# Matmuls in another order, and three sums of squares through short matmuls, in a one-core hybrid trunk

## What is computed

```python
def rms_norm(x, g):
    return x * lax.rsqrt(jnp.mean(x * x, axis=-1, keepdims=True) + NORM_EPS) * g

def sqrelu_mlp(h, w_up, w_down):            # 2048 -> 8192 -> 2048
    return jnp.square(jax.nn.relu(h @ w_up)) @ w_down

h = x
for layer in range(2):
    hn = rms_norm(h, mix_norm[layer])
    mix = attention(hn, ...) if layer == 0 else rglru_block(hn, ...)
    h = h + mix
    h = h + sqrelu_mlp(rms_norm(h, mlp_norm[layer]), w_up[layer], w_down[layer])
return rms_norm(h, final_norm)
```

## Time and profile before

| | us |
|---|---|
| median of 3 runs | 1996.98 (1996.09 to 1997.16) |
| profiled execution | 1997.17 |
| its span, first to last instruction | 1995.2 |
| PE busy | 1981.6 (99%), 11532 matmuls |
| PE weight loads busy | 1735.6 (87%), 11532 |
| DVE busy | 1368.6 (69%) |
| ACT busy | 1062.1 (53%) |
| mean granted TensorE clock | 0.999 of full speed |

### The profile page before, as it was taken

One profiled execution on the slowest core, in us unless ns is written; L12 is line 12 of the kernel. 1 busy time (PEld: TensorE's weight loads), 2 busy tenths in 40 slices (PEclk: granted clock), 3 DMA queues, 4 the chain that ended last, 5 costly groups with the idle time before them and its releaser, 6 DMA issues.

```text
span 1995.2 us, 33969 instructions
## 1 busy us (share of the span) xinstructions
PE 1981.6 (99%) x11532; PEld 1735.6 (87%) x11532; DVE 1368.6 (69%) x1575; ACT 1062.1 (53%) x1446; POOL 7.3 (0%) x11
## 2 busy tenths in 40 slices
PE   9999999999999999999999999999999999999998
PEld 8898888888888888888888888888888888888887
DVE  7998676556656665666789997766566556656664
ACT  6666554444444444445588885544444444444453
POOL 1000000000000000000000000000000000000000
PEclk9999999999999999999999999999999999999999
DMA  8544565666555656556566655555665566555652
GB/s 286 158 127 153 175 200 185 195 187 191 188 187 177 198 188 189 178 179 200 190 190 189 189 169 188 191 190 189 191 188 184 195 180 198 186 188 177 199 175 95
DMA packets 365307, 368.17 MB, mean 185 GB/s; under 512 B 11472, under 2 KB 363856, under 8 KB 365136
## 3 DMA queue, kind: packets, MB, share of 16 engines
q1 hardware_dynamic: 364976, 365.53, 58.1%
q0 software_dynamic: 288, 2.10, 0.3%
HBM read 365.48 MB, written 2.10 MB: 184 GB/s over the span
## 4 chain that ended last, share of the span: by engine, by line
PE 94%; DVE 3%; ACT 2%; issue 1%; DMA 0%; DVEq 0%; SPq 0%; ACTq 0%
PE ps L1307 61%; PE ps L1310 30%; DVE w_lo L812 1%; ACT h L467 1%; PE aux L1327 1%; PE aux L1328 1%; PE aux L1329 1%; ACT w_hi L370 0%; DVE h L923 0%; DMA h<-x_l_dram 0%; DVE h L934 0%; PE aux L1382 0%; DVE u L826 0%; DVE pt L939 0%; DVE u L899 0%
## 5 line engine op out<-in xcount | busy, mean ns | idle before, releaser
L812 DVE TENSOR_TENSOR w_lo<-w_raw,w_hi 128x1024 fp32r<-128x1024 f32 x678 | 815.7, 1222 | 337.8 <-ACT w_hi L370 336.7
L370 ACT ACTIVATE w_hi<-w_raw 128x1024 fp32r<-128x1024 f32 x678 | 701.3, 1053 | 449.9 <-PE ps L1310 446.8
L1307 PE MATMUL ps<-xn,w_hi 128*128 128x512 f32 x2880 | 907.5, 396 | 2.5 <-DVE xn L880 2.3
L1307 PE MATMUL ps<-mid,w_hi 128*128 128x512 f32 x2544 | 799.4, 396 | 1.0 <-DVE w_lo L812 0.5
L1310 PEld LDWEIGHTS ps<-xn,w_lo 128*128 128x128 f32 x2880 | 541.7, 188 | 128.2
L1310 PEld LDWEIGHTS ps<-mid,w_lo 128*128 128x128 f32 x2544 | 477.9, 188 | 113.0
L1310 PE MATMUL ps<-xn,w_lo 128*128 128x256 f32 x2880 | 566.8, 278 | 0.0
L1310 PE MATMUL ps<-mid,w_lo 128*128 128x256 f32 x2544 | 500.1, 278 | 0.0
L1307 PEld LDWEIGHTS ps<-xn,w_hi 128*128 128x128 f32 x2880 | 439.6, 189 | 3.5 <-issue 2.9
L1307 PEld LDWEIGHTS ps<-mid,w_hi 128*128 128x128 f32 x2544 | 387.2, 189 | 1.8 <-DVE w_lo L812 0.9
L826 DVE TENSOR_TENSOR u<-ps,half 128x512 f32<-128x512 f32 x169 | 116.5, 690 | 155.3 <-ACT half L383 136.0
(11 more groups left out here) (168 smaller groups left out, 757.4 us busy)
## 6 DMA issues: line engine op xcount, KB each, us to landing
w_raw<-mlp_w_up_dram SPq DMA_DIRECT2D x256, 512.0 KB, 3.8
w_raw<-mlp_w_down_dram SPq DMA_DIRECT2D x256, 512.0 KB, 3.6
w_raw<-b_w_in_dram SPq DMA_DIRECT2D x64, 512.0 KB, 4.9
w_raw<-a_w_qkv_dram SPq DMA_DIRECT2D x40, 512.0 KB, 5.5
w_raw<-a_w_o_dram SPq DMA_DIRECT2D x32, 512.0 KB, 4.6
w_raw<-b_w_out_dram SPq DMA_DIRECT2D x32, 512.0 KB, 4.8
h<-x_l_dram SPq DMA_DIRECT2D x4, 512.0 KB, 8.6
gate_raw<-b_gate_a_w_dram SPq DMA_DIRECT2D x8, 256.0 KB, 2.8
```

The costliest lines, as they stand in the source:

```text
L370: nc.scalar.activation(w_hi[:, s, :, :], w_raw[:, slot, :, :], ACT.Copy).then_inc(hi_ready, 1)
L812: nc.vector.tensor_tensor(w_lo[:, s, :, :], w_raw[:, slot, :, :], w_hi[:, s, :, :].bitcast(F32), ALU.subtract).then_inc(lo_ready, 1)
L1307: nc.tensor.matmul(ps[:, 2 * half_i + b, :], hi[:, k, b * PART:(b + 1) * PART], operand[:, :, kt, :], start=kt == 0, stop=False)
```

## The change

In products a flag in_turn gives another order: for b = 0, for all four k, long and then short, and then the same for b = 1. It is set for all chunks of both MLPs but the first pair of each, for all chunks of the recurrent quads 1 to 7, and for chunks 0 to 2 of six attention pairs. All other chunks keep the order.

stats(n) is replaced by short_stats(n) for n = 1, 2 and 3 (both MLP norms and the recurrent block's norm); stats(0) stays. For it ScalarE copies acc to the high part of xc_split and VectorE subtracts to get the low part, both behind the first split of the pair (next_hi and next_lo with s = 0), and TensorE multiplies a float32r matrix of ones, ones_r, with the two parts of the two halves, four matmuls of 256 columns. GpSimd sets ones_r in a third memset, for which TensorE's first loop waits as well.

```diff
             nc.gpsimd.memset(eps[:, :], EPS).then_inc(consts_set, 1)
+            nc.gpsimd.memset(ones_r[:, :].bitcast(F32), 1.0).then_inc(consts_set, 1)
...
+            def acc_split_hi(n):
+                act.wait_ge(acc_ready, 8 * (n + 1))
+                nc.scalar.activation(xc_split[:, 0, :, :], acc[:, :, :], ACT.Copy).then_inc(acc_hi, 1)
+
             def up_step(q, half_i, j, relus, norm=None):
-                for s in range(3):
+                next_hi(q, half_i, 0)
+                if norm is not None:
+                    acc_split_hi(norm)
+                for s in (1, 2):
                     next_hi(q, half_i, s)
...
+            def acc_split_lo(n):
+                dve.wait_ge(acc_hi, n)
+                nc.vector.tensor_tensor(xc_split[:, 1, :, :], acc[:, :, :], xc_split[:, 0, :, :].bitcast(F32),
+                                        ALU.subtract).then_inc(acc_lo, 1)
...
-            def products(q, half_i, s, operand, ready_sem, ready, late=False):
+            def products(q, half_i, s, operand, ready_sem, ready, late=False, in_turn=False):
...
-                for k in range(CH_KT):
+                def long(k, b):
                     kt = s * CH_KT + k
-                    for b in range(2):
-                        nc.tensor.matmul(ps[:, 2 * half_i + b, :], hi[:, k, b * PART:(b + 1) * PART],
-                                         operand[:, :, kt, :], start=kt == 0, stop=False)
-                    for b in range(2):
-                        last = nc.tensor.matmul(ps[:, 2 * half_i + b, TOK:2 * TOK], lo[:, k, b * PART:(b + 1) * PART],
-                                                operand[:, 0, kt, :], start=False, stop=kt == KT - 1)
+                    nc.tensor.matmul(ps[:, 2 * half_i + b, :], hi[:, k, b * PART:(b + 1) * PART],
+                                     operand[:, :, kt, :], start=kt == 0, stop=False)
+
+                def short(k, b):
+                    kt = s * CH_KT + k
+                    return nc.tensor.matmul(ps[:, 2 * half_i + b, TOK:2 * TOK], lo[:, k, b * PART:(b + 1) * PART],
+                                            operand[:, 0, kt, :], start=False, stop=kt == KT - 1)
+
+                if in_turn:
+                    for b in range(2):
+                        for k in range(CH_KT):
+                            long(k, b)
+                            last = short(k, b)
+                else:
+                    for k in range(CH_KT):
+                        long(k, 0)
+                        long(k, 1)
+                        short(k, 0)
+                        last = short(k, 1)
                 last.then_inc(wts_used, 1)
...
+            def short_stats(n):
+                pe.wait_ge(acc_lo, n)
+                for b in range(2):
+                    nc.tensor.matmul(x3[:, 0:TOK], ones_r[:, :], xc_split[:, 0, b, :], start=b == 0, stop=False)
+                    last = nc.tensor.matmul(x3[:, 0:TOK], ones_r[:, :], xc_split[:, 1, b, :], start=False, stop=b == 1)
+                last.then_inc(stats_done, 1)
...
-            pe.wait_ge(consts_set, 2)
+            pe.wait_ge(consts_set, 3)
...
-                pair(q, half_i, *qkv, between)
+                pair(q, half_i, *qkv, between, (0, 1, 2) if g_before is not None else ())
...
-                quad(base, *operand, {3: lambda: stats(norm)})
+                whole = tuple(range(CHUNKS))
+                quad(base, *operand, {3: lambda: short_stats(norm)}, (), whole)
                 with pe.Fori(1, 4) as i:
-                    quad(i + base, *operand)
+                    quad(i + base, *operand, None, whole)
...
-            quad(QB_IN, *lru_in, {3: lambda: stats(2)})
+            quad(QB_IN, *lru_in, {3: lambda: short_stats(2)})
             with pe.Fori(1, GATE_BLOCKS) as n:
-                quad(n + QB_IN, *lru_in, {0: lambda: gates(n - 1)})
+                quad(n + QB_IN, *lru_in, {0: lambda: gates(n - 1)}, tuple(range(CHUNKS)))
```

More of the change, by code:

```diff
@@ L154, in build @@
         ones = sb("ones", [PART, PART])
+        ones_r = sb("ones_r", [PART, PART], F32R)
         eps = sb("eps", [PART, 1])
@@ L224, in build @@
         consts_set = sem("consts_set")
+        acc_hi, acc_lo = sem("acc_hi"), sem("acc_lo")
         stats_done, rms_ready = sem("stats_done"), sem("rms_ready")
@@ L698, in lru_quad @@
                 next_hi(q, 0, 0)
+                if isinstance(n, int) and n == 0:
+                    acc_split_hi(2)
                 if before:
@@ L1044, in _ @@
                 residual_step(i + QB_WO, 1, i * 2 + 1, (1, "mlp0"))
+            def acc_split_lo(n):
+                dve.wait_ge(acc_hi, n)
+                nc.vector.tensor_tensor(xc_split[:, 1, :, :], acc[:, :, :], xc_split[:, 0, :, :].bitcast(F32),
+                                        ALU.subtract).then_inc(acc_lo, 1)
             def up_step(q, half_i, j, relus, norm=None):
-                for s in range(3):
+                next_lo(q, half_i, 0)
+                if norm is not None:
+                    acc_split_lo(norm)
+                for s in (1, 2):
                     next_lo(q, half_i, s)
@@ L1197, in lru_quad @@
                 next_lo(q, 0, 0)
+                if isinstance(n, int) and n == 0:
+                    acc_split_lo(2)
                 if before:
@@ L1312, in products, with pair, quad @@
                 last.then_inc(wts_used, 1)
-            def pair(q, half_i, operand, ready_sem, ready, between=None):
+            def pair(q, half_i, operand, ready_sem, ready, between=None, in_turn=()):
                 for s in range(CHUNKS):
-                    products(q, half_i, s, operand, ready_sem, ready)
+                    products(q, half_i, s, operand, ready_sem, ready, in_turn=s in in_turn)
                     if between and s in between:
                         between[s]()
-            def quad(q, operand, ready_sem, ready, between=None, between_b=None):
-                pair(q, 0, operand, ready_sem, ready, between)
-                pair(q, 1, operand, ready_sem, ready, between_b)
+            def quad(q, operand, ready_sem, ready, between=None, in_turn=(), in_turn_b=None):
+                pair(q, 0, operand, ready_sem, ready, between, in_turn)
+                pair(q, 1, operand, ready_sem, ready, None, in_turn if in_turn_b is None else in_turn_b)
@@ L1446, in mlp @@
                 operand = (xn, xn_ready, 8 * norm)
-                quad(base, *operand, {3: lambda: stats(norm)})
+                whole = tuple(range(CHUNKS))
+                quad(base, *operand, {3: lambda: short_stats(norm)}, (), whole)
                 with pe.Fori(1, 4) as i:
-                    quad(i + base, *operand)
+                    quad(i + base, *operand, None, whole)
                 with pe.Fori(0, 4) as i:
-                    quad(i + (base + 4), mid, mid_ready, mid_base)
+                    quad(i + (base + 4), mid, mid_ready, mid_base, None, whole)
                 with pe.Fori(1, GROUPS) as g:
                     with pe.Fori(0, 4) as i:
-                        quad(g * 8 + i + base, *operand)
+                        quad(g * 8 + i + base, *operand, None, whole)
                     with pe.Fori(0, 4) as i:
-                        quad(g * 8 + i + (base + 4), mid, mid_ready, g * PAIRS + mid_base)
+                        quad(g * 8 + i + (base + 4), mid, mid_ready, g * PAIRS + mid_base, None, whole)
             mlp(QB_MLP0, 1, MID_MLP0)
```

## The result

The changed kernel takes 2015.37 us (median of 4 runs, 2014.38 to 2015.57), the kernel before in the same session 1997.07: the ratio is 1.0091 with a 95% interval of 1.0079 to 1.0104. It is slower by 18 us, where the forecast was 1995.8 and the range ended at 2008.

The account below looks back on a forecast made before the run. TensorE's matmul stream was taken to bound the kernel. From the profiled 1997.17 us, order zero, sums -1.14 and start zero gave 1996.0, or 1995.8 against the median; own range 1993 to 2001, whole range 1967 to 2008.

Parts of the forecast that it names:

- What bounds the kernel: TensorE's stream: matmuls busy 99% of the span, PE never waits, 1 ns in a group of four matmuls is 2.3 us.
- One surcharge of 13 to 14 ns per matmul, wherever it stands: Every matmul costs that over its columns, whatever its neighbours, so the new order changes nothing: zero; chance 0.42.
- The range of that step: Bounds on the new order's effect: 14 ns a group down (32 us) to 10 ns a group up (23 us).
- the upper case: The new order is slower, 8 ns a group (2014) or 10 ns (2019); chance 0.19.
- Rival A: Alternating long and short saves 7 ns a group, 16 us, giving 1980; chance 0.39.
- Rival B: Eight matmuls in a row into one PSUM bank cost 8 ns a group, 18 us, giving 2014; chance 0.19.
- The sums: Short float32r sums of squares in three norms save 0.38 us each, 1.14 us in all, with their operand's preparation hidden.
- The start: An added memset delays the warm-up 0.1 to 0.2 us, hidden; the half clock could shift -1.7 to +1.7 us; taken as zero.
- The rule on the ports: Skill rule: weight loads take no bandwidth from the running matmul; estimates a group at 650 ns where the trace has 697.

Follow-up runs that it names:

- e7: Changed kernel with eight longs, then eight shorts, in every in-turn chunk of the first MLP and only the first in-turn chunk of the second; 2006.81 us.
- e5: Changed kernel plus short matmuls in the gates' form and operands behind the sums of squares, 24 in the first MLP, 6 in the second; 1992.03 us.
- e8: Changed kernel plus six short matmuls of the gates' form behind the sums of squares of both MLPs; 1989.81 us, ratio 0.9967 to the kernel before.
- e14: Changed kernel with only eps and ones_r exchanged in memory, so ones_r starts at 32 within 64 bytes; 1987.45 us, ratio 0.9956 to the kernel before.
- e4: Changed kernel with in-turn chunks ordered by k and then b, so a bank gets two matmuls in a row, not eight; 2014.41 us.
- e3: Changed kernel with the old order of matmuls everywhere, the short sums of squares alone; 1996.15 us, ratio 0.9995 to the kernel before.
- e2: Changed kernel with the float32 sums of squares of before, the new order alone; 2016.24 us, ratio 1.0098 to the kernel before.
- e9: Changed kernel plus 24 short matmuls behind each MLP's sums, weights always ones_r in the first MLP, one tile of gate_hi in the second; 2008.0 us.
- e13: Changed kernel with ones_r and eps exchanged in memory, plus 24 short matmuls on ones_r behind the second MLP's sums; 1990.47 us.
- e11: Kernel before with 32 unused bytes ahead of w_hi, so w_hi and w_lo lie apart from xn and mid; 2011.8 us, ratio 1.0075.
- e6: Changed kernel with 4 of 24 gate matmuls per recurrent quad, plus 24 shorts per MLP, weights gate_hi in the first, ones_r in the second; 2005.21 us.
- e15: e14 with the new order in 64 more chunks: output projections, first pairs of the MLPs, first recurrent quad; 1987.92 us, ratio 0.9958 to the kernel before.
- e10: Changed kernel with the old order in both MLPs; 1995.43 us, ratio 0.9991 to the kernel before.
- e1: Changed kernel plus 24 short matmuls on ones_r and xc_split behind the sums of squares of both MLPs; 2021.16 us, ratio 1.0121 to the kernel before.

## Why the prediction was wrong, step by step

*What bounds the kernel: right.* PE's stream sets the time, nothing hides a difference in it, 1 ns in a group is 2.3 us. The loss is the spacing of 504 chunks.

*"One surcharge of 13 to 14 ns per matmul, wherever it stands ... I take zero": this step failed.* It was a fit of one constant to two mixtures, and I treated the 4 ns a group by which they didn't fit as rounding. The constant holds for longs in a row, for shorts in a row and for the fast alternation (e7: 0.227 and 0.120, that is 14 and 13 ns over the columns). It doesn't hold for the slow one, where a group costs 0.7067 and not 0.6933. In its place: the spacing of one and the same stream takes two values, and which one depends on what ran ahead; in the MLPs, adding six or 24 shorts (e5, e8) or moving the sums' weights by 32 bytes (e14) changed it from slow to fast.

*The range of that step was built for it, and still missed.* The 10 ns a group at the upper end are just what was measured (0.7067 - 0.6967). That they met is luck: they stood for a short's 0.120 in a run. And I gave the upper case 0.19 and cut the range at half of it.

*Rival A, 1980: a fast spacing exists, but the row didn't show it.* It is there in 73 chunks of the changed kernel, and with the entry mended (e14) in 577 of 578. Its price is 3.4 ns a group, not 7. The 7 ns were mostly rounding. In the trace of before the run starts and ends at:

```profile
59.84 0.28 PE L1327 MATMUL aux<-kpad,qz 128*128 128x256 f32 x1
...
62.71 0.62 PE L1307 MATMUL ps<-xn,w_hi 128*128 128x512 f32 x2
```

It takes 2.87 us and not the 24 x 0.120 = 2.88 that I subtracted, and the two groups of the earlier trace rows take 0.69 (59.15 to 59.84) and 0.70 (62.71 to 63.41), like all others. That alternation has a fast spacing at all, for a rival built on this, is luck.

*Rival B, 2014: the right time by the wrong mechanism.* 2014 lies 1.4 us under the result, and the sign of what decides it (over 0.6985) came true. But e4 changes the banks and nothing happens, and the recurrent stage is fast with eight in a row in one bank. So the near hit is luck. I had read the run's 0.120 against 0.116 as a price of the bank; in e7, with the bank changed at every short, eight shorts in a row have 0.120 too.

*What the trace of before already showed.* In it a chunk of the old order at 191 us takes 2.774 and the one behind it 2.799, with the same instructions as all others at 2.787. So the spacing of one stream can differ from chunk to chunk with nothing but its past. The prediction read a steady stretch, 503 to 700 us, and not this one.

*The sums: right.* 1.14 worked out, 1.2 by the medians of e3 (not clear of noise by its interval) and 0.9 by e2 against the changed kernel, in two sessions. The copy went in behind the second w_hi at 266.92 (worked out: 267.3, from the trace of before, whose stage begins 0.3 later), the operand had 2.2 us of cover.

*The start: right within its bounds.* PE's first loop starts at 1.25 for 1.11 and the wait for xn shrinks from 2.26 to 1.95. The half clock came in some executions and not in others: see below.

*The rule on the ports.* I had set the Trainium skill ("TensorE: Matmul & The Clock Gate", Part 2: two independent read ports, so the next weights' load takes nothing from the running matmul) against the 57 ns of a group. The runs speak against it again: e9 and e13 move only the place of a run's weights, and a short goes from 0.1167 to 0.120 us (with e7 both at 0 within 64 bytes, 0.120 too). How the two reads lie to each other matters, so they are not independent in this stream. Why apart is cheaper in a run while the pad of e11, with every instruction the same, costs 0.024 us a chunk is not known. That the reads of the two ports collide is my reading; no run shows the collision itself.

*Open.* What the state is that lasts over hundreds of microseconds. It has more than two values, since the first recurrent chunk is slow behind a fast MLP in e8 and fast behind one in e5, with the same matmuls between. Shorts that lie alike lead to the fast spacing in all MLP entries of e5, e8, e13 and e14 and don't in e7, in e6's first recurrent quad and in e15's; no run varied the number of shorts at an entry step by step, or what stands ahead of them, with all places held. Other distances than 0 and 32 within 64 bytes weren't tried.

## What to carry to other kernels

Where an engine is never idle, a steady stream of its instructions may have more than one spacing; compare the same code in two stages of one trace before pricing a change of order. When a change of order is slow in one place and fast in another, look at what runs just ahead and at where the operands lie within 64 bytes: here exchanging two small tensors turned +0.9% into -0.4%. Measure such an exchange and don't rely on it as a rule: the same four matmuls led to either spacing in e15. And a constant that fits two mixtures to 1 ns a matmul is no proof where the question is 2 ns a group.

## What the runs showed of the hardware that I had not expected

- The same alternation of long and short float32r matmuls at full clock runs at 0.3467 or 0.3533 us a pair for hundreds of microseconds. In the MLPs a change to the 4 to 28 matmuls ahead switched it (changed kernel, e5, e8, e14); what ran before those counts as well (e6, e15, the first recurrent chunk).
- Short matmuls in a row take 0.120 us each where weights and moving operand start alike within 64 bytes, 0.1167 where they start 32 bytes apart (e9, e13). With 32 bytes ahead of w_hi, which also moves what lies behind it, the old order went from 2.787 to 2.811 us a chunk (e11).
- The stretch of half clock near 11 to 14 us comes in some executions of a kernel and not in others. In e3's profiled execution it is missing, with the same PE loop and a like wait for xn; e3's times fall into two heaps, near 1995.0 and near 1996.2 us, as do those of the kernel before (1996.2 and 1997.4). The ten kernels with four or more executions agree: where the profiled one had the stretch its time is in the upper heap (before, changed, e10), where it had not, in the lower (e1, e2, e3, e8, e11, e14, e15). So differences of about 1 us between medians can be a matter of heaps.
  The stretch of e3's profiled execution (busy by engine with counts, granted clock, DMA share, GB/s):

```profile
11.00:15.00 4.00, 4.00 (x23) 3.39 (x22) 3.93 (x9) 3.86 (x9) 0.00 (x0) 1.00 1.05 380
```
